# Long convolutions of a Hyena branch: pairs of planes on half arrays, the complex product summed on GpSimd

## The reference, cut to what matters

```python
def bidir_long_conv(u, h_fwd, h_bwd):
    k = jnp.concatenate([h_fwd[:1] + h_bwd[:1], h_fwd[1:], jnp.zeros_like(h_fwd[:1]),
                         jnp.flip(h_bwd[1:], axis=0)], axis=0)
    u_f = jnp.fft.rfft(u, n=2 * seqlen, axis=1)
    k_f = jnp.fft.rfft(k, n=2 * seqlen, axis=0)
    return jnp.fft.irfft(u_f * k_f[None], n=2 * seqlen, axis=1)[:, :seqlen]

for o, gate in enumerate((x1, x2)):
    z = gate * (bidir_long_conv(z, filt[:, 0, o], filt[:, 1, o]) + h_bias[o] * z)
```

## Time and profile before

| what | value |
|---|---|
| median of three runs | 3736.09 us (3731.5 to 3737.49) |
| span of the profiled execution | 3733.1 us |
| mean granted TensorE clock | 0.957 of full speed |
| TensorE matmul / weight load busy | 3404.8 us (91%) / 2819.8 us (76%) |
| VectorE, ScalarE, GpSimd busy | 2317.8 us (62%), 1527.0 us (41%), 1890.6 us (51%) |
| DMA | 622.32 MB, 167 GB/s in the mean |
| long convolutions | from 2024 to 2661 us |

### The profile page before, as it was taken

How to read it: one execution, slowest core, us unless ns; L and a number is a source line. 1 busy time by engine, 2 the same in 40 slices (tenths; PEclk the granted TensorE clock), 3 DMA queues, 4 the chain that set the end, 5 groups by cost and what they waited for, 6 DMA issues and landing times. The chain is left out here.

```text
span 3733.1 us, 45021 instructions
## 1 busy us (share of the span) xinstructions
PE 3404.8 (91%) x16246; PEld 2819.8 (76%) x16246; DVE 2317.8 (62%) x2902; ACT 1527.0 (41%) x2965; POOL 1890.6 (51%) x1146
## 2 busy tenths in 40 slices
PE   6899999996999999977898999999577997999998
PEld 2778888885888888855896888887466886788886
DVE  5786885226878852227443666776496886667662
ACT  3433223334332233332675455554345663333332
POOL 0487998776869987731000101100168873445442
PEclk8999999997999999988999999999788998999998
DMA  7544333333342333248997867856475555465552
GB/s 260 165 144 148 113 110 116 113 112 109 124 136 104 111 121 109 109 170 355 276 298 219 174 158 162 184 133 163 114 304 174 174 168 192 161 212 195 188 190 101
DMA packets 403760, 622.32 MB, mean 167 GB/s; under 512 B 154444, under 2 KB 241404, under 8 KB 400500
## 3 DMA queue, kind: packets, MB, share of 16 engines
q1 hardware_dynamic: 303069, 428.06, 37.6%
q10 hardware_dynamic: 91256, 157.83, 11.4%
q0 software_dynamic: 9216, 33.56, 4.0%
HBM read 416.34 MB, written 203.03 MB: 166 GB/s over the span
## 5 line engine op out<-in xcount | busy, mean ns | idle before, releaser
L751 PE MATMUL pl_bank<-hl_hi,pl_a_hi 128*128 128x512 f32 x2056 | 813.4, 396 | 41.3 <-DVE hl_lo L374 28.8
L753 PE MATMUL pl_bank<-hl_hi,pl_a_lo 128*128 128x512 f32 x2056 | 804.8, 391 | 0.0
L752 PE MATMUL pl_bank<-hl_lo,pl_a_hi 128*128 128x512 f32 x2056 | 804.4, 391 | 0.0
L696 POOL TENSOR_TENSOR pl_a_lo<-pl_sums,pl_a_hi 128x512 fp32r<-128x512 f32 x288 | 436.7, 1528 | 119.0 <-ACT pl_a_hi L800 119.0
L751 PEld LDWEIGHTS pl_bank<-hl_hi,pl_a_hi 128*128 128x128 f32 x2056 | 388.3, 189 | 128.5 <-DVE hl_lo L374 28.8
L753 PEld LDWEIGHTS pl_bank<-hl_hi,pl_a_lo 128*128 128x128 f32 x2056 | 388.4, 189 | 82.4
L752 PEld LDWEIGHTS pl_bank<-hl_lo,pl_a_hi 128*128 128x128 f32 x2056 | 389.0, 189 | 78.0
L800 ACT ACTIVATE pl_a_hi<-pl_sums 128x512 fp32r<-128x512 f32 x288 | 181.8, 633 | 540.2 <-PE pl_bank L753 480.8
L2099 POOL TENSOR_TENSOR mo_w_lo<-mo_w,mo_w_hi 128x1024 fp32r<-128x1024 f32 x96 | 237.9, 2481 | 280.7 <-ACT mo_w_hi L2170 280.6
L696 POOL TENSOR_TENSOR pl_a_lo<-hl_w,pl_a_hi 128x512 fp32r<-128x512 f32 x220 | 310.7, 1426 | 114.1 <-ACT pl_a_hi L800 113.9
L2127 PE MATMUL mo_bank<-mo_hi,mo_w_hi 128*128 128x512 f32 x768 | 305.4, 398 | 23.3 <-POOL mo_w_lo L2099 18.6
(11 more groups left out here) (247 smaller groups left out, 6944.6 us busy)
## 6 DMA issues: line engine op xcount, KB each, us to landing
hl_w<-in_w_rec SPq DMA_DIRECT2D x146, 512.0 KB, 3.3
conv_spec<-spec_s SPq DMA_DIRECT2D x248, 256.0 KB, 6.3
mo_w<-in_w_br SPq DMA_DIRECT2D x96, 512.0 KB, 3.8
kern_s<-taps_res SPq DMA_DIRECT2D x16, 2048.0 KB, 7.0
spec_xin<-kern_s SPq DMA_DIRECT2D x64, 512.0 KB, 5.5
spec_s<-spec_res ACTq DMA_DIRECT2D x128, 256.0 KB, 4.1
g_s<-pl_res ACTq DMA_DIRECT2D x32, 512.0 KB, 2.6
conv_gin<-u_s POOLq DMA_DIRECT2D x32, 512.0 KB, 7.1
```

The source lines that it names most:

```text
L696: nc.gpsimd.tensor_tensor(a_lo[:, at % NS, :], src, a_hi[:, at % NS, :].bitcast(F32), ALU.subtract).then_inc(s_lo, 1)
L751: pe.matmul(out, a_hi[:, q, m], op_hi[:, b, k, :], start=begin, stop=False)
L752: pe.matmul(out, a_hi[:, q, m], op_lo[:, b, k, :], start=False, stop=False)
L753: return pe.matmul(out, a_lo[:, q, m], op_hi[:, b, k, :], start=False, stop=end)
```

## The change

In the plane loop, two planes make a pair h (16 pairs).

- `forward(j, h)` makes four matmuls of 64 output columns, for a in (real, imaginary) and pl in (first, second plane). Plane 0 of the pair goes to PSUM partitions 0 to 63, plane 1 to 64 to 127; real parts lie in the first 256 columns of the bank, imaginary parts in the last 256.
- VectorE multiplies the whole bank by the real and the imaginary spectrum in one instruction (`product`, 128x1024); the first pair, with plane 0, takes two instructions and its own buffer `edge`. A spectrum is loaded once, not for both halves of the partitions (128 KB a transfer where 256 KB were).
- GpSimd makes the sum and the difference (`both`), two instructions of 128x256 for a pair.
- `inverse(j, h)` makes four matmuls with 64 rows each (plane 0 from partitions 0 to 63, plane 1 from 64 to 127), to two banks of `inv`, with one table `wv` in the place of `wi` and `wj`. It runs one group of two pairs (`LAG` = 2) behind `forward`.
- ScalarE copies two planes in one instruction (128x512).
- The loads of `x` move from GpSimd to SP, between the spectra; the gates' loads and the stores move to ScalarE's queue. SP has 5 small transfers for `edge` at each convolution.

```diff
@@ phase_long_convs
+            def load_edge(j, s):
+                if j:
+                    sp.wait_ge(s_p, NH * (j - 1) + 1)
...
+                for h in range(NH):
+                    s = spec_v[o * NBK + blk, h]
+                    if h == 0:
+                        load_edge(j, s)
+                    else:
+                        m = plain(j, h)
+                        if m >= SLOT:
+                            sp.wait_ge(s_p, NH * ((m - SLOT) // (NH - 1)) + (m - SLOT) % (NH - 1) + 2)
+                        for k in range(2):
+                            sp.dma_start(spec[k * NA:(k + 1) * NA, m % SLOT], s[k]).then_inc(s_k[m % SLOT], 16)
+                    if h % 4 == 3:
+                        if j == 0:
+                            load_x(1, h // 4)
+                        elif convs[j - 1][1] == 1 and convs[j - 1][0] < 2:
+                            sp.wait_ge(s_st, 64 * (convs[j - 1][0] + 1))
+                            load_x(convs[j - 1][0] + 2, h // 4)
...
+            for n in range(NH * NV):
+                q = n % PS
+                pool.wait_ge(s_p, n + 1)
+                if n >= PS:
+                    pool.wait_ge(s_v, n - PS + 1)
+                nc.gpsimd.tensor_tensor(both[:, q, 0], prod[:, q, 0, 0], prod[:, q, 1, 1], ALU.subtract).then_inc(s_w, 1)
+                nc.gpsimd.tensor_tensor(both[:, q, 1], prod[:, q, 0, 1], prod[:, q, 1, 0], ALU.add).then_inc(s_w, 1)
...
-                pe.matmul(bank[ubank[k % 4]][:, 0:CB], wf[:, k, :], y[:, k, :], start=True, stop=True).then_inc(s_u, 1)
...
-                pe.matmul(out, wi[:, k, :], prod[:, n % 4, 0, :], start=True, stop=False)
-                pe.matmul(out, wj[:, k, :], prod[:, n % 4, 1, :], start=False, stop=True).then_inc(s_v, 1)
+                for a in range(2):
+                    for pl in range(2):
+                        mm = pe.matmul(ubank[h % 4][pl * NA:(pl + 1) * NA, a * CB:(a + 1) * CB],
+                                       wf[:, 2 * h + pl, a * NA:(a + 1) * NA], y[:, 2 * h + pl, :], start=True, stop=True)
...
+                for a in range(2):
+                    pe.wait_ge(s_w, 2 * n + a + 1)
+                    for pl in range(2):
+                        rows = slice(pl * NA, (pl + 1) * NA)
+                        mm = pe.matmul(inv[:, 2 * (h % 2) + pl, 0:CB], wv[rows, h, a, :], both[rows, n % PS, a, :], start=(a == 0), stop=(a == 1))
...
+                    for h in range(0, NH + LAG, 2):
+                        if h < NH:
+                            forward(j, h)
+                            forward(j, h + 1)
+                        if h >= LAG:
+                            inverse(j, h - LAG)
+                            inverse(j, h - LAG + 1)
...
-                        nc.scalar.copy(v[:, :, k], bank[2 + k % 2][:, 0:CB]).then_inc(s_vm, 1)
+                        nc.scalar.copy(v[:, :, 2 * h:2 * h + 2].rearrange("p c k -> p k c"),
+                                       inv[:, 2 * (h % 2):2 * (h % 2) + 2, 0:CB]).then_inc(s_vm, 1)
+                        if j and h < 2:
+                            store(j - 1, 2 + h)
+                        if h == 2:
+                            for c in range(3):
+                                load_gate(j, c)
```

More of the change, by code:

```diff
@@ L1218, in phase_long_convs @@
     NQ, NR, SLOT = 16, 8, 4
+    NH, LAG, PS = NPL // 2, 2, 4
     with ExitStack() as ctx:
         ph = Phase(nc, "conv", ctx)
-        fx, wf, wi, wj, back, ident = (tables[n] for n in ("fx", "wf", "wi", "wj", "back", "ident"))
+        fx, wf, wv, back, ident = (tables[n] for n in ("fx", "wf", "wv", "back", "ident"))
         x = ph.sb("x", [P, 2, NG, NA])
@@ L1230, in phase_long_convs @@
         back_hi, back_lo = ph.sb("back_hi", [P, 2, P], F32R), ph.sb("back_lo", [P, 2, P], F32R)
-        bank = banks(ph, 8)
+        front = [ph.ps(f"front{b}", [P, 512]) for b in range(2)]
+        inv = ph.ps("inv", [P, 4, 512])
+        extra = [ph.ps(f"extra{b}", [P, 512]) for b in range(2)]
+        ubank = (*extra, *front)
         s_x, s_g, s_k = [ph.sems(f"x{b}", 4) for b in range(2)], ph.sems("gate_in", 3), ph.sems("k", SLOT)
+        s_edge, s_zero = ph.sem("edge_in"), ph.sem("zero")
         s_a, s_ea, s_ev = ph.sem("first"), ph.sem("ev_act"), ph.sem("ev_dve")
-        s_u, s_p, s_v, s_vm = ph.sem("u"), ph.sem("prod"), ph.sem("inv"), ph.sem("inv_out")
+        s_u, s_p, s_w, s_v, s_vm = ph.sem("u"), ph.sem("prod"), ph.sem("both"), ph.sem("inv"), ph.sem("inv_out")
         s_bh, s_bl, s_tl = ph.sem("back_hi"), ph.sem("back_lo"), ph.sem("turned_lo")
@@ L1248, in _ @@
         @block.sync
         def _(sp):
[L1250 to L1265, removed]
@@ L1267, in _ @@
-        @block.gpsimd
-        def _(pool):
-            def load_x(blk, c):
[L1270 to L1283, removed]
+            def load_x(blk, c):
+                sp.dma_start(x[:, blk % 2, 16 * c:16 * (c + 1), :], u_v[0][blk, :, 16 * c:16 * (c + 1), :]
+                             ).then_inc(s_x[blk % 2][c], 16)
@@ L1326, in turn @@
                 if q == 0:
[L1327 removed]
+                    pe.wait_ge(s_vm, NH * (j + 1))
                 if q >= 2:
@@ L1382, in _ @@
                 if j < NV:
-                    for k in range(NPL + 2):
-                        if k < NPL:
-                            forward(j, k)
-                        if k >= 2:
-                            inverse(j, k - 2)
+                    for h in range(0, NH + LAG, 2):
[5 more added lines that the diff above has]
+                            inverse(j, h - LAG + 1)
         def take(eng_op, q, part, g):
```

138 lines of the change are left out of this document (80 added, 58 removed).

## The result

| | median us | lowest to highest | runs |
|---|---|---|---|
| before | 3734.44 | 3731.5 to 3737.49 | 4 |
| changed | 3692.46 | 3687.89 to 3696.76 | 4 |

The ratio is 0.9879, with a 95% interval from 0.9863 to 0.9895: the changed kernel is 1.2% faster, 42 us where 73 were forecast. Its profiled execution has a span of 3690.1 us, 43.0 less than before.

A forecast was written before the change was run, and what follows sets the result against it. TensorE bounds the plane loops by the columns it streams. Terms -83 - 10 + 20 + 5 - 4 - 1 = -73 from the profiled 3733.1 us give 3660, as a median 3663 us; range 3628 to 3785.

The forecast's parts named there:

- Two halves at once, 0.215 us a matmul: TensorE in plane loops: half-array matmuls run two at once, 0.215 us each, 1.72 for a pair where 2.58 was.
- A change of halves, 0.15 us: TensorE, each group of two pairs: switching between column and row halves costs 0.15 us, bounds 0 to 0.28.
- The other engines: Per pair, VectorE, GpSimd and ScalarE stay below TensorE's 1.87 us, hidden; rival GpSimd bound: 3716 us, chance 0.07.
- One loop, 31.0 us: Plane loop from first `forward`: 30.2 us plus 0.8 for handoffs at the start, 31.0 against 41.9.
- The failed step: ScalarE's queue: 48 transfers cost 0, hidden by idle time; without it half a microsecond each.
- SyncE's wait, +20: Convolutions 3 and 4: SP's load of `x` waits for stores, spectra queue behind it; 10 us lost, twice.
- the clock, +5: Convolutions 3 and 4: TensorE idles about 9 us in each, so its granted clock falls, 2.5 us each.
- The old excess, -10: Plane loops: of 13.3 us excess over 42.8, half the bytes for spectra save 10 us.
- Start and end, -4: Wait for the first `x`, issued on SP instead of GpSimd, with the end's stores: -4 us (0 to -7).
- table, -1: One table of 2048 KB less on a busy queue, mostly beside other work: -1 us (0 to -3).
- loops -83: Eight plane loops, each 10.4 us shorter after a last copy 0.5 us longer: -83 us.
- The rivals without overlap and with half of it: Plane loops: no overlap, 0.43 us a matmul, 3872 us, chance 0.12; half overlap, only rows or columns, 3766 us, chance 0.12.

The follow-up runs named there:

- the one-half run: Inverse's matmuls all on rows 0 to 63, second plane's sums left out, against the 3631 us version (gates on GpSimd, later x loads): 3728.76 us, ratio 0.9972.
- the version with free queues: Not defined by this name; apparently gates' loads moved from ScalarE's queue to GpSimd's, against the changed kernel: 3646.40 us, ratio 0.9753.

## Why the prediction was right or wrong

The sign, the range and the main mechanism held; the size did not, by 29 us. One step failed by 46 us, and it is in part luck that the miss is smaller: the rest of the loops came out 9 us better than their terms, and the part ahead of the loops 7 us better.

- **Two halves at once, 0.215 us a matmul**: right, shown by the one-half run (2.00 against 3.72 us). A group takes 3.81 us, 3.74 forecast.
- **A change of halves, 0.15 us**: 0.18 measured. The Trainium skill (TensorEngine Tiling (Array Packing), Key Properties) says that a change of mode drains TensorE, by which 0 was out; the 0.18 us agrees.
- **The other engines**: sums 0.73 us (0.74), product 1.22 (1.21), copy 1.06 (1.1). GpSimd did not become the bound, and the product, with GpSimd busy 22.3 us of a loop beside it, isn't stretched.
- **One loop, 31.0 us**: 31.1 once ScalarE's queue is free, in six of eight loops. In the changed kernel none reached it.
- **The failed step: "ScalarE's queue takes 48 transfers, six at most in a stage where it is busy under half the time: 0, hidden by that idle time; without it half a microsecond each."** I took the mean busy share of ScalarE as cover, and the price of one issue. But three are issued in one go in the loop, and together they take 4.4 to 10.5 us, not 1.5; with a copy every 1.9 us (3.81 for two) and banks for two pairs, ScalarE can be late by some 2 us, an estimate from the code (in the rows of convolution 1 it was 4.5 us late and TensorE waited 2.73). Measured price of the gates' loads on this queue: 46 us, of which some 10 are the clock that falls once TensorE has stood still. 36 of the 46 lie in the six loops where TensorE waited for the copy; the 9.8 in loops 3 and 4 are a later spectrum, a cost that the forecast didn't have at all. Idle time covers a wait only if no single one is longer than the buffers reach.
- **SyncE's wait, +20, and the clock, +5**: 25 forecast, 20.0 measured with ScalarE's queue free (loops 3 and 4 at 42.5 and 42.1 against 32.3). 1.8 and 2.6 us of this are the clock (32.64 and 33.35 us busy less 30.80), where 2.5 each were forecast, so 15.6 are left for the wait. The chain was right: in loop 3 of the version with the gates on GpSimd the last store is issued at 6.1 us (7.2 forecast) and lands at 12.2 (12.3), and the spectrum has landed at 17.8 (18.5). The remainder after moving the wait, 4 us each, isn't the wait but 2 MB of `x` that must come within a loop that also loads 4 MB of spectra, which I had not looked at. In the changed kernel the lower clock costs 14.8 us over eight loops, most of it as a follower of the failed step.
- **The old excess, -10**: right in direction. In the version with free queues only loops 3 and 4 stay longer, so all 13.3 were there to gain.
- **Start and end, -4; table, -1**: together -12.0 up to the first `forward`. The wait for the first `x` fell from 15.5 to 10.4 us, and the table's absence gave 5.9, where I had 1; the load was not hidden beside other work. What it delayed on its way there I did not trace.

Against the sum: loops -83, -10, +20 and +5 are -68, and the version with the gates on GpSimd has -77.3 there, of which -83, -13.3 and +20.0 explain 76.3; the changed kernel has the 46 us of the gates' loads on top. The rivals without overlap and with half of it are excluded by the group of 3.81 us.

## What to carry to other kernels

An engine's idle share does not cover work put on its queue: compare the longest single stretch that the engine is held with what the buffers behind it can bridge, and spread transfers over the loop instead of issuing them in a row. When TensorE is made faster, the same bytes come in less time, so look at the DMA's busy slices in each loop, and move loads into the empty ones. A probe that forces both halves onto one is a cheap proof of where an overlap's gain comes from.

## What the runs showed that was not expected

- Issues in a row on ScalarE's queue, of 512 KB each in packets of 256 bytes, cost 0.37 us for the first (1.1 and 2.6 in two of eight loops), 1.4 to 2.8 for the second and 2.1 to 5.0 for the third; one issued alone, 5 pairs apart, 0.37. It is not ScalarE's alone: in the changed kernel SyncE's first four loads of `x`, of the same size, take 0.36, 1.43, 2.12 and 2.35 us in a row.
- The same load takes 1.15 us of GpSimd each time, also three in a row (3.45), and travels in larger packets (613 under 512 bytes in a loop instead of 12840), yet the loop's spectra came no sooner (median landing 5.2 us, against 4.1).
- Matmuls on two halves overlap although the program lists both of one half first (inferred from starts and durations); the order costs 0.15 us in 3.8.
- With the inverse's overlap gone TensorE is busy all the time and its clock stays full; in the changed kernel it falls to 0.85 to 0.95, in seven of the eight loops where it waited.
